# Recurrence of the second block: row maxima as one product of stacked high and low rows, turns ahead of the last values, norm in two batches

## What is computed

```python
qkm = silu(causal_short_conv(concat([qm, km]), w_conv, b_conv))
log_i = ig + b_igate ; log_f = log_sigmoid(fg + b_fgate)      # one row of 512 per head
# stabilised mLSTM; b is the running sum of log_f
log_d = b[t] - b[s] + ic[s]                                   # causal
m_t   = maximum(m_inter, max(log_d))
s_qk  = (q @ k.T) * exp(log_d - m_t)
h     = (s_qk @ v) / maximum(abs(sum(s_qk)), exp(-m_t))
hm    = sigmoid(og) * rms_norm(h)                             # per head
x     = x + gate * (concat([attn, hm]) @ w_out)
```

## Time and profile before

| | us |
|---|---|
| runs before | 2113.51, 2113.75, 2109.97 |
| median | 2113.51 |
| the profiled execution, its own time | 2114.27 |
| its span (first to last instruction) | 2112.2 |
| TensorE busy in the span | 2085.9 |
| mean granted TensorE clock, share of full | 0.993 |

### The profile page before, as it was taken

The page is one execution under the profiler, slowest core; times in us unless marked ns, Lnnn a source line. Parts: engine busy times, 40 slices in busy tenths (PEclk is TensorE's granted clock), DMA queues, the critical chain, the costliest instruction groups (busy, mean ns, idle before and its releaser), DMA issues.

```text
span 2112.2 us, 27482 instructions
## 1 busy us (share of the span) xinstructions
PE 2085.9 (99%) x9816; PEld 1705.1 (81%) x9816; DVE 975.7 (46%) x1723; ACT 673.1 (32%) x919; POOL 964.3 (46%) x712
## 2 busy tenths in 40 slices
PE   7999999999999999999999999999999999999999
PEld 5888778888888878877788888888978777888887
DVE  4677335545353636843456355357254463111111
ACT  4123443322122322244443222134356333222221
POOL 4445325455554444542455455553433134545444
PEclk9999999999999999999999999999999999999999
DMA  5332122344342232222134344322221112222222
GB/s 183 97 105 100 60 80 90 120 160 159 126 155 97 101 114 94 100 81 80 60 110 159 140 159 141 133 84 94 92 89 61 60 60 80 96 90 94 100 100 100
DMA packets 35561, 222.13 MB, mean 105 GB/s; under 512 B 5236, under 2 KB 5620, under 8 KB 9720
## 3 DMA queue, kind: packets, MB, share of 16 engines
q1 hardware_dynamic: 27728, 189.80, 25.9%
q10 hardware_dynamic: 7720, 30.78, 4.2%
HBM read 215.59 MB, written 2.10 MB: 103 GB/s over the span
## 4 chain that ended last, share of the span: by engine, by line
PE 96%; DVE 2%; issue 1%; DMA 1%; ACT 0%; DVEq 0%; SPq 0%; ACTq 0%
PE ps L364 25%; PE ps L365 24%; PE ps L366 24%; PE ps L381 3%; PE ps L382 3%; PE ps L383 3%; PE ps L449 2%; PE ps L411 1%; PE ps L413 1%; PE ps L412 1%; PE ps L459 1%; PE ps L470 1%; DMA w_raw<-in_weights 1%; PE ps L502 1%; PE ps L740 0%
## 5 line engine op out<-in xcount | busy, mean ns | idle before, releaser
L335 POOL TENSOR_TENSOR w_lo<-w_raw,w_hi 128x512 fp32r<-128x512 f32 x708 | 964.1, 1392 | 1135.2 <-ACT w_hi L843 1135.2
L364 PE MATMUL ps<-a_hi,w_hi 128*128 128x512 f32 (+1 forms) x1560 | 613.8, 393 | 0.0
L366 PE MATMUL ps<-a_hi,w_lo 128*128 128x512 f32 (+1 forms) x1560 | 608.2, 390 | 0.0
L365 PE MATMUL ps<-a_lo,w_hi 128*128 128x512 f32 (+1 forms) x1560 | 608.0, 390 | 0.0
L843 ACT ACTIVATE w_hi<-w_raw 128x2048 fp32r<-128x2048 f32 x177 | 338.9, 1915 | 780.9 <-PE ps L366 669.5
L364 PEld LDWEIGHTS ps<-a_hi,w_hi 128*128 128x128 f32 (+1 forms) x1560 | 291.6, 187 | 68.4 <-issue 7.2
L366 PEld LDWEIGHTS ps<-a_hi,w_lo 128*128 128x128 f32 (+1 forms) x1560 | 291.7, 187 | 63.5 <-issue 0.6
L365 PEld LDWEIGHTS ps<-a_lo,w_hi 128*128 128x128 f32 (+1 forms) x1560 | 291.9, 187 | 60.4 <-issue 0.4
L366 PE MATMUL ps<-b_hi,w_lo 128*128 128x512 f32 x612 | 238.1, 389 | 0.0
L364 PE MATMUL ps<-b_hi,w_hi 128*128 128x512 f32 x612 | 238.1, 389 | 0.0
L365 PE MATMUL ps<-b_lo,w_hi 128*128 128x512 f32 x612 | 238.1, 389 | 0.0
(11 more groups left out here) (278 smaller groups left out, 2439.9 us busy)
## 6 DMA issues: line engine op xcount, KB each, us to landing
w_raw<-in_weights SPq DMA_DIRECT2D x177, 1024.0 KB, 4.9
v<-in_ada ACTq DMA_DIRECT2D x24, 1024.0 KB, 4.9
x<-in_x_in SPq DMA_DIRECT2D x4, 512.0 KB, 9.6
out<-x SPq DMA_DIRECT2D x8, 256.0 KB, 2.0
yc<-in_c_rows ACTq DMA_DIRECT2D x2, 512.0 KB, 3.2
bias<-in_mult_bias ACTq DMA_DIRECT2D x1, 640.0 KB
cs_rope<-in_rope ACTq DMA_DIRECT2D x1, 512.0 KB, 7.8
g<-q ACTq DMA_DIRECT2D x16, 32.0 KB, 4.7
```

Source lines behind the costliest of these rows:

```text
L335: nc.gpsimd.tensor_tensor(w_lo[:, s, piece], w_raw[:, s, piece], f32(w_hi[:, s, piece]), ALU.subtract).then_inc(w_lo_ready, 1)
L364: nc.tensor.matmul(o, wh, hi(kt), start=kt == 0, stop=False)
L365: nc.tensor.matmul(o, wh, lo(kt), start=False, stop=False)
L366: last = nc.tensor.matmul(o, wl, hi(kt), start=False, stop=kt == depth - 1)
```

## The change

What it does:

- Row maxima: ScalarE rounds `row_g` to a high part (rows 0 to 3 of `row_parts`), VectorE writes the rest to rows 32 to 35, the selector has ones for both, and one float32r product of 36 rows gives their sum. Two ScalarE copies of 36 x 512 fill the operands at tile 23, one of 4 x 512 at tile 27; VectorE's subtraction stands at tile 28.
- The turns and the maxima of heads 0 and 1 (now banks 3 and 2) go ahead of the last `values`.
- ScalarE makes `y_hi` of the last pair straight from bank 7, and VectorE `y_lo` too, between `m_gaps(0)` and `m_gaps(1)`.
- `m_products(0)` follows the last `values` at once; `attended(0)` and `attended(1)` come behind it.
- The norm runs for heads 0 and 1, and then for 2 and 3; the turns of heads 0 and 1 stand ahead of `attended(5)`, those of 2 and 3 behind `attended(7)`. The weight split of block `C_OUT + 2` stands behind the first square root on ScalarE.

```diff
-        mrows = sb("mrows", [MH, 2, S])
+        mrows = sb("mrows", [F_ROW + MH, 2, S])
...
+        row_parts, sel_parts = (b_hi[0:F_ROW + MH, e, :] for e in range(2))
...
-        m_bank, m_pr = (ps[7][:, :], ps[2][:, :], ps[7][:, :], ps[7][:, :]), (pr, bias)
+        m_bank, m_pr = (ps[3][:, :], ps[2][:, :], ps[7][:, :], ps[7][:, :]), (bias, pr)
...
+            def a_turns():
+
+                pe.wait_ge(pt_ready, nth(L, HEADS, HEADS - 1))
+                pe.wait_ge(m_exp, 1)
+                pe.wait_ge(m_rows, 1)
...
+            def m_maxima(h):
+
+                if h == 0:
+                    pe.wait_ge(row_split, 1)
+                if h < 2:
+                    b = (3, 2)[h]
+                    pe.wait_ge(bank_free[b], nth(L, LAYER_TILES // 4, SECOND_BANKS[:T_OUT].count(b)))
+                else:
+                    pe.wait_ge(m_gap, h)
+                nc.tensor.matmul(m_bank[h], sel_parts[:, h * P:(h + 1) * P], row_parts,
+                                 start=True, stop=True).then_inc(m_bc, 1)
...
+                        if pair == AT:
+                            a_turns()
+                            m_maxima(0)
+                            m_maxima(1)
                         values(L, pair - 1)
...
-            pe.wait_ge(pair_copied, nth(L, AT, AT - 1))
-            m_maxima(0)
-            attended(0)
             pe.wait_ge(mc_silu, 2 * MH)
             pe.wait_ge(mv_ready, 1)
             pe.wait_ge(a_cols, 1)
             m_products(0)
-            for b in (2, 3):
-                pe.wait_ge(bank_free[b], nth(L, LAYER_TILES // 4, SECOND_BANKS[:T_OUT].count(b)))
-            m_maxima(1)
+            attended(0)
             attended(1)
...
-            attended(5)
-            for h in range(MH - 1):
-                m_turn(h)
-            attended(6)
-            attended(7)
-            m_turn(MH - 1)
+            m_turn(0)
+            m_turn(1)
+            for n in range(5, KT):
+                attended(n)
+            m_turn(2)
+            m_turn(3)
...
+                        nc.scalar.activation(row_parts[0:MH, :], row_g, ACT.Copy).then_inc(row_hi, 1)
                         nc.scalar.activation(row_e, row_b, ACT.Exp, scale=-1.0).then_inc(m_exp, 1)
                     if t == 2 * C_VM + 1:
+                        act.wait_ge(y_split, nth(L, AT, 1))
+                        nc.scalar.activation(sel_parts, sel, ACT.Copy)
+                        nc.scalar.activation(row_parts, sel, ACT.Copy)
...
+            act.wait_ge(pair_done, nth(L, AT, AT - 1))
+            nc.scalar.activation(y_hi[:, AT - 1, :], ps[7][:, :], ACT.Copy).then_inc(y_hi_ready, 1)
             for h in range(MH + 2):
                 if h < MH:
                     act.wait_ge(m_gap, h + 1)
                     nc.scalar.activation(m_pr[h % 2][:, :], m_pr[h % 2][:, :], ACT.Exp, scale=-1.0).then_inc(m_decay, 1)
-                if h == MH + 1:
-                    m_sqrt(0, slice(0, MH - 1))
                 if h >= 2:
                     m_taken(h - 2)
                 if h == MH:
+                    m_sqrt(0, slice(0, 2))
                     act.wait_ge(tile_done, nth(L, LAYER_TILES, T_OUT + 3))
                     w_split(L, C_OUT + 2)
...
+                    if t == 2 * C_VM + 6:
+                        dve.wait_ge(row_hi, 1)
+                        tt(row_parts[F_ROW:F_ROW + MH, :], row_g, f32(row_parts[0:MH, :]), ALU.subtract
+                           ).then_inc(row_split, 1)
...
+            m_gaps(0)
+            dve.wait_ge(y_hi_ready, nth(L, AT, AT - 1))
+            tt(y_lo[:, AT - 1, :], ps[7][:, :], f32(y_hi[:, AT - 1, :]), ALU.subtract).then_inc(y_split, 1)
+            m_gaps(1)
...
             for h in range(MH):
+                if h == MH - 1:
+                    m_means(slice(0, 2))
...
+                if h == MH - 1:
+                    m_inverse(0, slice(0, 2))
+                    m_scaled(0)
+                    m_scaled(1)
...
+            dve.wait_ge(og_ready, 1)
+            m_gated(0)
+            m_gated(1)
+            late = slice(2, MH)
+            m_means(late)
             attended(5)
-            m_gated(0)
-            m_means(late)
             m_low(0)
             m_inverse(1, late)
-            m_scaled(MH - 1)
-            m_gated(1)
+            m_scaled(2)
+            m_scaled(3)
+            m_low(1)
             attended(6)
-            m_low(1)
-            m_gated(2)
             attended(7)
-            m_low(2)
-            m_gated(MH - 1)
-            m_low(MH - 1)
+            for h in range(2, MH):
+                m_gated(h)
+            for h in range(2, MH):
+                m_low(h)
...
-        selectors[h, h * P:(h + 1) * P] = 1.0
+        selectors[h, h * P:(h + 1) * P] = selectors[F_ROW + h, h * P:(h + 1) * P] = 1.0
```

More of the change, by code:

```diff
@@ L234, in two_blocks @@
         og_ready = sem("og_ready")
+        row_hi = sem("row_hi")
+        row_split = sem("row_split")
         f_ready = sem("f_ready")
@@ L280, in two_blocks @@
         tri = cs_rope[:, 1, 0:P]
-        sel, iw_rows = mrows[:, 0, :], mrows[:, 1, :]
-        row_a, row_b, row_e, row_g = g[0:MH, 6, :], g[0:MH, 7, :], mrows[:, 1, :], rms[0:MH, :]
+        sel, iw_rows = mrows[:, 0, :], mrows[0:MH, 1, :]
+        row_a, row_b, row_e, row_g = g[0:MH, 6, :], g[0:MH, 7, :], mrows[0:MH, 1, :], rms[0:MH, :]
+        row_parts, sel_parts = (b_hi[0:F_ROW + MH, e, :] for e in range(2))
         key_bank = (ps[4][:, :], ps[5][:, 0:384], ps[6][:, 0:256], ps[5][:, 384:512])
@@ L681, in qk_turn @@
                 last.then_inc(qn_turned, 1)
+            def a_turns():
+                pe.wait_ge(pt_ready, nth(L, HEADS, HEADS - 1))
+                pe.wait_ge(m_exp, 1)
+                pe.wait_ge(m_rows, 1)
+                for e, rows in enumerate((row_a, row_e)):
+                    for tt in range(TT):
+                        c = 2 * P + MH * (TT * e + tt)
+                        last = nc.tensor.transpose(ps[6][:, c:c + MH], rows[:, tt * P:(tt + 1) * P], ident[0:MH, 0:MH])
+                last.then_inc(a_turned, 1)
+            def m_maxima(h):
[8 more added lines that the diff above has]
+                                 start=True, stop=True).then_inc(m_bc, 1)
             for j in range(C_OUT):
@@ L719, in _ @@
                             transposes(L, 2 * pair + part - 2)
[L722 to L735, removed]
             def m_products(h):
@@ L1096, in _ @@
                         nc.scalar.activation(row_e, row_e, ACT.Ln, bias=1.0).then_inc(f_log, 1)
-                    if part == 0 and 1 <= pair <= AT:
+                    if part == 0 and 1 <= pair < AT:
                         pair_out(L, pair - 1)
@@ L1137, in _ @@
             m_high(0)
-            m_sqrt(1, slice(MH - 1, MH))
-            for h in range(1, MH):
+            m_high(1)
+            m_sqrt(1, slice(2, MH))
+            for h in range(2, MH):
                 m_high(h)
@@ L1591, in qk_norm, with m_gaps @@
                                                ).then_inc(qk_normed, 1)
+            def m_gaps(h):
+                dve.wait_ge(m_bc, h + 1)
+                for i in range(TT):
+                    nc.vector.tensor_scalar(m_pr[h % 2][:, TRT[i]:TRT[i + 1]], m_bank[h][:, i * P:],
+                                            acol[:, 0, i, h:h + 1], 0.0, ALU.subtract, ALU.max)
+                dve.drain().then_inc(m_gap, 1)
             for j in range(C_OUT):
@@ L1647, in _ @@
                                                        ).then_inc(mc_silu, 1)
-                    if part == 0 and 1 <= pair <= AT:
+                    if part == 0 and 1 <= pair < AT:
                         y_low(L, pair - 1)
             dve.wait_ge(a_turned, 1)
-            nc.vector.tensor_copy(acol[:, :, :, :].rearrange("p e a b -> p (e a b)"), ps[6][:, 0:2 * TT * MH]
-                                  ).then_inc(a_cols, 1)
+            nc.vector.tensor_copy(acol[:, :, :, :].rearrange("p e a b -> p (e a b)"),
+                                  ps[6][:, 2 * P:2 * P + 2 * TT * MH]).then_inc(a_cols, 1)
             dve.drain()
[L1655 to L1663, removed]
+            m_gaps(0)
+            dve.wait_ge(y_hi_ready, nth(L, AT, AT - 1))
+            tt(y_lo[:, AT - 1, :], ps[7][:, :], f32(y_hi[:, AT - 1, :]), ALU.subtract).then_inc(y_split, 1)
+            m_gaps(1)
             def m_mask(h):
@@ L1902 @@
     t = np.arange(P)
-    selectors = np.zeros((MH, MH * P), np.float32)
+    selectors = np.zeros((F_ROW + MH, MH * P), np.float32)
     for h in range(MH):
-        selectors[h, h * P:(h + 1) * P] = 1.0
+        selectors[h, h * P:(h + 1) * P] = selectors[F_ROW + h, h * P:(h + 1) * P] = 1.0
     arrays = {
```

2 lines of the change are left out of this document (removed).

## The result

| | before | after |
|---|---|---|
| median of 5 runs, us | 2113.51 | 2101.09 |
| lowest and highest | 2109.97 to 2116.48 | 2100.87 to 2103.99 |
| profiled execution, own time | 2114.27 | 2100.94 |
| its span | 2112.2 | 2098.8 |
| mean granted clock | 0.993 | 0.997 |

The ratio is 0.9944, 95% interval 0.9933 to 0.9955: 12.4 us faster, give or take 2.3. The forecast was 2101.3.

A forecast was written before the change was run, and what follows sets the result against it. TensorE bounds the kernel (96% of the chain): 45.6 us of stage work plus about 1.1 us of waiting starts the tile pair 12.2 us sooner, taking the 2113.51 median to 2101.3 us, range 2098.5 to 2106.5.

The forecast's parts named there:

- The sum: TensorE's work from the last values to the tile pair at full clock: 45.6 us, tile pair at most 13.3 us sooner.
- the last wait: Before the tile pair, TensorE waits about 1.1 us for the bank of attended(7), behind the norm's second batch.
- The turns of the heads: Sixteen transposes of m_turn on TensorE, some 0.42 us per four from start to start, 1.7 us in all.
- my list: Split of the 13.3 us at most: 4.2 idle, 5.3 clock, 3.3 maxima, 0.5 changes between kinds of work.
- The start: At the stage's start, y_lo ends at 1663.8, attended(0) wants it at 1664.4; nothing to 0.1 left of the 0.99 us wait.
- The decay of head 0: Before m_values(0): factors ready at 1668.6, TensorE occupied until 1670.2, so 0.83 us of idle and the half clock go.
- The rows for the maxima: Ahead of the first maximum: row_split expected ready at about 1650.5, 9 us before it is wanted at 1659.4.
- The rival of a slower kernel: Maxima ahead of values wait for a late row_split and hold up the stage: 2118 us and up, chance 0.02.
- The end: From m_values(3) to the tile pair: scalings by 1693.8 or 1694.9, bank 1 free at 1705.3, tile pair 12.2 us sooner.
- the third rival: Waits inside the stage stay in part, late y_lo or first turns, with half-clock stretches: 5.4 us back, 2106.7, chance 0.17.
- The clock: In the stage, half-clock stretches that lost 5.3 us go; no drop likelier behind the 1.1 us wait, one priced at 1.7.
- my own sign: Forecast is wrong if the stage is outside 44 to 52 us or what follows the tile pair changes length.

The follow-up runs named there:

- the second float32 profile: Changed kernel with the maxima back as float32 products of 4 rows, profiled again: one execution of 2103.84 us, stage 49.53 us.
- the experiment through `q`: Changed kernel with y_hi and y_lo of the last pair made from a copy in q instead of straight from bank 7: median 2102.35 us.
- the kernel with one more operation: Changed kernel with one unused VectorE operation of 0.7 us added ahead of the last two additions to x: median 2102.33 us.

## Why the prediction was right

- **The time.** The mechanism was right in most of its steps, but that the forecast of 2101.3 came within 0.2 us is luck: the interval of the difference is 2.3 us either way, the stage got 11.8 us shorter and not 12.2, and the rest came from parts of the program that I took as unchanged.
- **The sum.** Forecast: TensorE's own work 45.6 us, plus 1.1 us of waiting, a tile pair 12.2 us sooner. Measured: 46.56 busy, 0.47 in the bracket, 11.8 us less stage. Two errors cancel in part: the work came out 1.0 too small and the last wait 0.6 too long. The maxima were mis-sized: 1.0 us for four, measured 0.66 + 0.43 + 0.43 = 1.5. A stacked maximum costs 0.33 to 0.43 us, not 0.25; that a change between kinds of work comes with each may be the reason, but no run isolates it. The turns of the heads are the second such term: 1.7 us forecast, 1.11 + 1.03 = 2.1 measured, 0.3 of it the wait inside them.
- **Where the 11.8 us come from.** TensorE's idle time fell from 4.35 to 0.56 us, 3.8 less. The maxima give 2.5, by the second float32 profile, and not the 3.3 of my list. The rest is 5.5; 5.3 of it is the clock, by the mean of 0.91 over 58.91 us, as I had put it.
- **The start.** `y_lo` was to end at 1663.8 and `attended(0)` to start at 1664.4. With the 0.44 us by which the stage starts earlier taken off, that is 1663.4 and 1664.0; measured 1663.2 and 1663.9. Taking the 0.75 us row of another operation with one PSUM operand was right, and the experiment through `q` shows the other bound.
- **The decay of head 0.** No bracket, as forecast.
- **The rows for the maxima.** I had `row_split` ready at about 1650.5; VectorE's subtraction ended at 1650.2, 8.5 us before the first maximum. The rival of a slower kernel had no part.
- **The end.** With the same 0.44 taken off, I had the two scalings until 1693.4, or 1694.5 if GpSimd got in between. It did, and they ended at 1695.05. So the turns of head 1, wanted at about 1694.8, waited 0.3 us: a small part of the third rival came true, without a half-clock stretch. I had two stands in the second `m_means`: there were two, but 0.65 and 1.17 us. Bank 1 came free at about 1705.2 instead of 1704.9, TensorE was done with its turns 1.0 us later than in my sum (1704.8 instead of 1703.8), and the wait was 0.47 instead of 1.1.
- **The clock.** I forecast none of the three half-clock stretches, and there is none. But the reason was wrong. I set the waits behind products of 4 rows, where the clock had fallen, against those behind full-size work, where I took no fall as likelier. The runs show neither kind to decide: a wait of 0.99 behind the maxima kept the clock in one kernel, 2.8 us behind full-size turns lost it in one of two executions. What the change does is to remove three waits behind which it fell; it can fall without one too, as the float32 maxima showed. So the forecast of a full clock in the stage rested on a rule that does not hold, and the one profile that I have of the changed kernel can't tell how often it comes true. The 5.3 us for the clock were the loss of one profiled execution, not a fixed cost. A coarse check from the runs: those of the kernel before with a mean clock of 0.997 took 2109.1 to 2109.7 us, those of the changed kernel with the same 0.997 took 2100.9 to 2101.1. Some 8 us of the 12.4 are there without a difference in the clock, to about 2 us, as the mean clock is rounded to 0.001.
- **Behind the stage** nothing should change, and 1.2 us did, in the clock's way back. By my own sign the forecast failed there; it is the spread between executions, which I had left out of that sign.

Why the single parts don't add up: the maxima alone gave 1.2 us of stage and cost 2.4 when taken back; the norm is worth 3.5 to 3.7 either way. The products in the place of `attended(0)` are worth 1.6, the place of the turns 0.5, the way of `y_lo` 0.7. The norm stands by itself. At the start of the stage the parts overlap: cheap maxima alone only lengthen the waits, and `attended(0)` no longer waits because the products stand in front of it, the turns stand ahead, and `y_lo` comes sooner.

## What to carry to other kernels

Sum the bound engine's own work from start to start at full clock, then walk the other engines' chains past it, one signal after another; both matter to 1 us here: the sum alone said 13.3 us, with the chains it was 12.2, and the stage gave 11.8. A cheaper operation ahead of a wait gives its gain to the wait, so shorten and reorder together. Let other ready work of the bound engine stand where a result is awaited, and charge a half-clock stretch to each wait that is left as a chance, not as a certainty.

## What the runs showed of the hardware

- The granted clock does not follow from the length of a wait. A wait of 0.99 us lost it and kept it (two kernels with the same order there), waits of 2.79 and 2.78 us kept it and lost it (the same kernel twice). Waits of 1.23 and 1.42 us kept it; waits of 0.79, 0.83, 1.46 and 1.62 lost it, and 1.96 lost it in all three kernels that have it. Each stretch at the lower level lost about 1.6 us. What decides stays open: each kernel has one or two profiles.
- It also falls with TensorE busy throughout. With float32 maxima it fell behind 2.4 us of small turns and 4-row products, in one of two executions. And there is a place ahead of the stage, the same work in every kernel: from 1460 to 1480 TensorE is busy 20.00 of 20 us in all fourteen profiles, and the mean clock is 1.00 in four, 0.91 in seven and 0.83 in three. Where it is 0.83 the stage starts at 1661.1 to 1661.6, elsewhere at 1657.7 to 1659.3. The row of the kernel with one more operation, in whose profile the clock falls at 1464, behind two-column products:

```profile
1460.00:1480.00 20.00, 20.00 (x96) 0.83 0.29 93
```

- Much of the spread between runs of one kernel goes with the clock: the kernel before took 2109.1 to 2116.7 us, at a mean clock of 0.997 in the fastest and 0.992 in the slowest. The changed kernel took 2100.9 to 2104.0 in its five runs (0.997 to 0.995). That it spreads less because its stage has fewer waits is not shown.
- A 4-row float32 product of 512 columns takes 1.05 us on TensorE, a 36-row float32r one 0.43, standing alone between other work.
